# Twenty-four attention steps, and the projections computed between them: single products or heads and rests

## The chip, the cores and the metric

The kernel runs on one core of one Trainium2 chip. The metric is the device time of one execution, in microseconds (us). The engines are named as the profile names them: PE is the matrix engine (TensorE), DVE the vector engine (VectorE), ACT the scalar engine (ScalarE), POOL is GpSimd, and SP (SyncE) issues most transfers. Each takes its own instructions in order, and they wait for each other through semaphores.

## What is computed

A decoder trunk of two layers over 512 rows of 1024 numbers. Only the first part of a layer, the mixer, is touched by the change. Cut to that:

```python
h = rms_norm(x, norm_mix[l])
z = h @ w_in[l]
(g_q, g_k, g_v, g_lr, g_r, d_q, d_k, d_v, i_q, i_k, i_w, c_u) = jnp.split(z, split_at, axis=-1)
o_gla  = rms_norm(gla_chunked(g_q, g_k, g_v, log_a), gla_onorm[l]) * jax.nn.silu(g_r)
o_dsa  = dsa_attention(rms_norm(d_q), rms_norm(d_k), d_v, i_q, i_k, i_w, rel_bias, topk)
o_conv = conformer_conv(c_u, ...)         # a * sigmoid(g), 31 taps over time, layer norm, silu
x = x + concatenate([o_gla, o_dsa, o_conv]) @ w_out[l]
```

After it come a cross-attention and a mixture of experts. `h @ w_in` is in float32. A product with float32 operands can be made directly, or from three products in the format fp32r. For that each operand is written as a head (its value copied to fp32r, by ACT) and a rest (value minus head, a subtraction); head times head, head times rest and rest times head are summed.

## The kernel before, in words

**The projections.** `w_in` is loaded in nine chunks (`CHUNKS`), three at a time in slots of `arena` (`chunk_at(n)` is slot n mod 3). A chunk is computed in jobs (`JOBS`), each with eight parts (c = 0 to 7, blocks of 128 of the 1024 inputs). Chunks 0 and 1 (the index keys and queries) are single float32 products with `hT`, the turned and normalised rows. Chunks 2 to 5 (`SPLIT`: dq, dk, dv, and g for gq and gk) are made from heads and rests: ACT writes the head of the rows `hT_head` and of each chunk `w_head` (`rows_head`, `chunk_head`), POOL subtracts (`rows_rest`, `chunk_rest`; the rest of a chunk takes the place of the chunk itself in its slot), and `split_project` gives PE three products a part. Chunks 6, 7 and 8 (ca and cg for the convolution and its gate; gv; gr, the gate of the linear attention) are single float32 products. `hT_head` lies where `x` was, so `x` is loaded again once chunk 5 is done (SP, L585).

**The steps.** The jobs of chunks 6 to 8 and the small jobs kt, upd and o of the linear attention aren't computed in one piece. They are spread, part by part, over the 24 steps of the sparse attention (4 tiles of rows by 6 heads). In step n PE turns the weights (`turn(n)`, L767), gives two parts, the products of a level of the linear attention (`level_product`, L692 and L707), in even steps the logits of steps n+2 and n+3 (`logits`, L758), the step's other parts, and `values(n-1)` (L776). DVE in its step n masks the logits of n+1 (`masked`, L1078), normalises n (`normalise`, L1088), merges a level, prepares the next (`differences` or `level_queries`), and does taps of the convolution (`conv_tap`, L1097 to L1100). `decay_to_end` (L1136) stands in step FACTORED and `factors` in the next. ACT does the exponentials and takes the jobs out of PSUM (`evacuate`). POOL adds bias and mask (`bm`, L1233 and L1234), up to two steps ahead, and multiplies the levels' keys (`level_keys`, L1223).

**What sets the order.** `LENGTH` holds an estimate for a part of each kind. The first four steps get 6.5 us of it each (`EARLY_US`), and the rest is spread evenly up to step 22. Which step a job ends in follows from this, and so do FACTORED and FIRST_TAP (the step after cg has ended); the taps are spread evenly from FIRST_TAP to step 21.

## Time and profile before

| | us |
|---|---|
| median of 3 runs | 1613.76 |
| lowest, highest | 1610.63, 1616.23 |
| profiled execution, device time | 1611.07 |
| its span in the profile | 1609.2 |
| PE, DVE, ACT, POOL busy | 1518.3, 1172.2, 848.5, 505.1 |
| mean granted clock of PE | 0.966 of full speed |

A busy time says how long an engine had something under way and not whether it bounds the kernel. A float32 product stands in the records as two matmuls. Brackets behind a row of the timeline give the idle time before it and who ended it. Layer 0 has its mixer from about 20 to 333 us, its steps from 150 to 310; layer 1 has the same steps from about 945 to 1107 us. Between the two lie the cross-attention and the experts.

### The profile page before, as it was taken

The page shows a single profiled execution, that of the slowest core. Times are in us where ns is not written, and L with a number is a line of the kernel's source. Part 1 is how long each engine was busy: PE and PEld are TensorE (multiplying, and loading weights), DVE is VectorE, ACT ScalarE, POOL GpSimd, SP SyncE. Part 2 cuts the span into 40 slices and gives each one's busy share as a digit, 9 for nine tenths or more (in the row PEclk, how much of TensorE's full clock was granted, in tenths as well). Part 3 has the DMA queues.
Part 4 walks back from the last instruction along what each step waited for, and adds up shares of the span by engine and source line. Part 5 has one row for each costly group of instructions (what it writes and reads, how often), then busy time and mean ns, then how long its engine had stood idle before and what let it go on. Part 6 is the DMA issues. An engine that isn't in the chain of part 4 may idle for free. (4 is left out here: it accounts for less than half of the span.)

```text
span 1609.2 us, 19743 instructions
## 1 busy us (share of the span) xinstructions
PE 1518.3 (94%) x6478; PEld 1044.6 (65%) x6478; DVE 1172.2 (73%) x1730; ACT 848.5 (53%) x1234; POOL 505.1 (31%) x224
## 2 busy tenths in 40 slices
PE   7999999999898999999899999999998899999996
PEld 3587565545566888877546865655455578877774
DVE  2697499541458999999837965985315599999997
ACT  4642323531537878788464513236125377788881
POOL 3043123100003666553532421321000036555444
PEclk9999989999979999999899999999998899999998
DMA  6243301314017999999641430103140289999994
GB/s 223 79 105 131 117 1 53 131 55 157 1 53 266 392 398 398 399 398 399 234 164 40 113 135 1 53 1 131 55 157 1 69 315 395 398 399 399 399 399 187
DMA packets 151769, 313.74 MB, mean 195 GB/s; under 512 B 33190, under 2 KB 46412, under 8 KB 151516
## 3 DMA queue, kind: packets, MB, share of 16 engines
q1 hardware_dynamic: 140300, 271.39, 46.5%
q0 software_dynamic: 6912, 25.17, 4.1%
q10 hardware_dynamic: 4496, 16.40, 2.5%
q8 instruction: 34, 0.56, 0.1%
q14 instruction: 27, 0.22, 0.0%
HBM read 288.81 MB, written 29.50 MB: 198 GB/s over the span
## 5 line engine op out<-in xcount | busy, mean ns | idle before, releaser
L1806 POOL TENSOR_TENSOR rest_w_down<-arena,head_w_down 128x2048 fp32r<-128x2048 f32 x30 | 189.1, 6304 | 193.8 <-ACT head_w_down L1955 193.8
L645 PE MATMUL ps<-hT,arena 128*128 128x512 f32 x352 | 162.8, 603 | 0.0
L2049 DVE TENSOR_TENSOR rest_w_down<-arena,head_w_down 128x2048 fp32r<-128x2048 f32 x30 | 150.5, 5018 | 14.8 <-ACT head_w_down L1955 14.7
L2049 DVE TENSOR_TENSOR rest_w_gate<-arena,head_w_gate 128x2048 fp32r<-128x2048 f32 x62 | 141.3, 2279 | 11.7 <-remote 11.7
L2049 DVE TENSOR_TENSOR rest_w_up<-arena,head_w_up 128x2048 fp32r<-128x2048 f32 x64 | 143.5, 2282 | 0.4 <-ACT head_w_up L1955 0.4
L1955 ACT ACTIVATE head_w_gate<-arena 128x2048 fp32r<-128x2048 f32 x60 | 114.8, 1918 | 41.4 <-DMA arena<-in_w_gate 40.6
L1955 ACT ACTIVATE head_w_down<-arena 128x2048 fp32r<-128x2048 f32 x60 | 115.0, 1925 | 39.5 <-DMA arena<-in_w_down 38.8
L1955 ACT ACTIVATE head_w_up<-arena 128x2048 fp32r<-128x2048 f32 x64 | 122.3, 1944 | 9.3 <-DMA arena<-in_w_up 9.2
L1740 POOL DMA_INDIRECT xg<-hrows,slot_tok x2 | 4.2, 2121 | 366.5 <-DVE slot_tok L1726 366.5
L1850 PE MATMUL ps<-head_w_gate,xg_head 128*128 128x512 f32 x256 | 105.6, 412 | 9.7 <-DVE xg_rest L2055 9.1
L645 PEld LDWEIGHTS ps<-hT,arena 128*128 128x128 f32 x352 | 63.9, 192 | 69.0 <-issue 68.1
L1850 PE MATMUL ps<-head_w_down,he_head 128*128 128x512 f32 x240 | 99.1, 413 | 5.4 <-DVE rest_w_down L2049 3.2
L1851 PE MATMUL ps<-rest_w_gate,xg_head 128*128 128x512 f32 x256 | 102.1, 399 | 0.0
L1852 PE MATMUL ps<-head_w_gate,xg_rest 128*128 128x512 f32 x256 | 101.8, 398 | 0.0
L1100 DVE SCALAR_TENSOR_TENSOR mixr<-arena,cf,mixr 128x512 f32<-128x512 f32 x120 | 98.4, 820 | 4.3
L1852 PE MATMUL ps<-head_w_up,xg_rest 128*128 128x512 f32 x256 | 99.7, 389 | 0.0
L1850 PE MATMUL ps<-head_w_up,xg_head 128*128 128x512 f32 x256 | 99.6, 389 | 0.0
L1851 PE MATMUL ps<-rest_w_up,xg_head 128*128 128x512 f32 x256 | 99.6, 389 | 0.0
L1852 PE MATMUL ps<-head_w_down,he_rest 128*128 128x512 f32 x240 | 94.1, 392 | 0.0
L1851 PE MATMUL ps<-rest_w_down,he_head 128*128 128x512 f32 x240 | 93.8, 391 | 0.0
L1963 ACT ACTIVATE xg_head<-ps,cf 128x128 fp32r<-128x128 f32 x256 | 69.2, 381 | 39.0 <-PE ps L1841 39.0
L1799 POOL DMA_INDIRECT xg<-hrows,idx x30 | 78.4, 2613 | 22.6 <-POOL idx L1812 22.6
(335 smaller groups left out, 3382.2 us busy)
## 6 DMA issues: line engine op xcount, KB each, us to landing
arena<-in_w_gate SPq DMA_DIRECT2D x64, 1024.0 KB, 10.3
arena<-in_w_up SPq DMA_DIRECT2D x64, 1024.0 KB, 11.0
arena<-in_w_down SPq DMA_DIRECT2D x64, 1024.0 KB, 10.4
arena<-in_w_in SPq DMA_DIRECT2D x10, 1536.0 KB, 6.7
yrows<-yb ACTq DMA_DIRECT2D x30, 512.0 KB, 6.3
arena<-in_w_in SPq DMA_DIRECT2D x4, 2048.0 KB, 7.8
x<-in_x SPq DMA_DIRECT2D x8, 512.0 KB, 13.9
arena<-in_w_in SPq DMA_DIRECT2D x16, 256.0 KB, 4.6
```

The lines of the kernel that those rows point to most:

```text
L645: last = nc.tensor.matmul(ps[n % 2][0:width, :], w[:, c, col:col + width], hT[:, c, :], start=(c == 0), stop=(c == KD - 1))
L1100: do(nc.vector.scalar_tensor_tensor(o, cin[:, i, j:j + S], convw[:, i, j:j + 1], o, ALU.mult, ALU.add))
L1740: gp.indirect_dma_start(out=xg[:, :], out_offset=None, in_=hrows, in_offset=bass.IndirectOffsetOnAxis(ap=slot_tok[:, 0:1], axis=0)).then_i ...
L1799: gp.indirect_dma_start(out=xg[:, :], out_offset=None, in_=hrows, in_offset=bass.IndirectOffsetOnAxis(ap=idx[:, :], axis=0)).then_inc(s_ga ...
L1806: nc.gpsimd.tensor_tensor(wl[2][:, c, :], raw[2][:, c, :], wh[2][:, c, :].bitcast(F32), ALU.subtract)\
L1850: nc.tensor.matmul(out, ah, bh, start=(c == 0), stop=False)
L1851: nc.tensor.matmul(out, ah, bl, start=False, stop=False)
L1852: last = nc.tensor.matmul(out, al, bh, start=False, stop=(c == n - 1))
L1955: nc.scalar.activation(wh[q][:, part(q, j), :], raw[q][:, part(q, j), :], ACT.Copy)\
L1963: last = nc.scalar.activation(xh[:, c, :], ps[4 + half][:, P * (c % 4):P * (c % 4) + P], ACT.Copy, scale=pc("gffn", c))
L2049: nc.vector.tensor_tensor(wl[q][:, c, :], raw[q][:, c, :], wh[q][:, c, :].bitcast(F32), ALU.subtract)\
```

## The change

Chunks 6, 7 and 8 are made from heads and rests too. For want of one large buffer their heads are made in seven pieces: ca, cg, gv_b (parts 5 to 7 of gv), gv_a (parts 0 to 4), gr0, gr1, gr2. Nothing is left in single float32 but chunks 0 and 1.

The rest of the rows is made twice: once as before (`hT_rest1`, for chunks 2 to 4), and once in two halves in the place of `hT` itself, for chunk 5 and later, since the first place is needed for heads. The heads of ca, cg and gv_b are made before the steps, gv_a's in step 1, gr0's in step 4, gr1's in step 10, gr2's in step 11; POOL makes the rests of the first three behind `bm` of step 1, and the others at its steps 5, 7, 13 and 15. `x` is loaded again only after the last part of gr, behind half of `w_out` instead of ahead of it. The lengths of parts become shorter, which moves jobs ahead: cg ends in step 3 (step 4 before), gv in step 9 (11 before), FACTORED and FIRST_TAP are 4 (5 before). Two idle products of PE ahead of layer 1 are gone.

```diff
-        SPLIT = [2, 3, 4, 5]
+        w_head = dict(dq=..., dk=..., dv=..., g=...,
+                      ca=heads_at("ca_head", place_of_sq, KD, CC), cg=heads_at("cg_head", soon, KD, CC),
+                      gv_a=heads_at("gv_head_a", place_of_sq, 5, GH * GV), gv_b=heads_at("gv_head_b", soon + 4 * KD * CC, 3, GH * GV),
+                      gr0=w_rest[8 % NSLOT][:, :, 384:512], gr1=heads_at("gr1_head", place_of_rs, KD, P),
+                      gr2=heads_at("gr2_head", place_of_sq, KD, P))
+        HEADS = ["rows", "dq", "dk", "dv", "g", "ca", "cg", "gv_b", "gv_a", "gr0", "gr1", "gr2"]
+        RESTS = ["rows1", "dq", "dk", "rows_a", "dv", "rows", "g", "ca", "cg", "gv_b", "gv_a", "gr0", "gr1", "gr2"]
...
-            LENGTH = dict(ca=0.87, cg=0.87, gr=0.87, gv=0.65, kt=0.6, upd=0.7, o=1.5)
+            LENGTH = dict(ca=0.69, cg=0.69, gr=0.69, gv=0.52, kt=0.6, upd=0.7, o=1.5)
+            VALUED, GATES = step_of(done("gv") - 1), step_of(done("gv") - 1) - 3
...
-                    sp.wait_ge(sN["proj_done"], BEFORE_STEPS)
+                    sp.wait_ge(sN["proj_done"], done("gr"))
                     for t in range(NT):
...
+                    def split_part(n, c):
...
+                        if c == 0:
+                            pe.wait_ge(sN["heads_in"], HEADS.index(of) + 1)
+                            pe.wait_ge(sN["rests_in"], RESTS.index(of) + 1)
...
+                        for a, (lhs, rhs) in enumerate(pairs):
+                            last = nc.tensor.matmul(o, lhs, rhs, start=(c == 0 and a == 0), stop=(c == KD - 1 and a == 2))
...
+                    def head(of, chunk, c=slice(0, KD), at=None):
...
+                        nc.scalar.activation(dst, chunk_at(chunk)[:, c, at], ACT.Copy).then_inc(sN["heads_in"], 1)
...
+                    rest("dk", 3)
+                    gp.wait_ge(sN["proj_done"], AFTER_IDX)
+                    rows_rest(hT_rest, slice(0, KD // 2))
+                    rest("dv", 4)
+                    rows_rest(hT_rest, slice(KD // 2, KD))
+                    rest("g", 5)
...
                         if n == 1:
+                            rest("ca", 6, at=slice(0, CC))
+                            rest("cg", 6, at=slice(CC, 2 * CC))
+                            rest("gv_b", 7, c=slice(5, KD))
...
+                        if n == 5:
+                            rest("gv_a", 7, c=slice(0, 5))
+                        if n == GATES + 1:
+                            rest("gr0", 8, at=slice(0, P))
+                        if n == VALUED + 4:
+                            rest("gr1", 8, at=slice(P, 2 * P))
+                        if n == VALUED + 6:
+                            rest("gr2", 8, at=slice(2 * P, 3 * P))
...
                         row_turned(pe, 3)
-                        idle_products(2)
```

DVE from the end of its step 4 into its step 5, which begins with the masking of step 6's logits. The line numbers of the changed kernel are higher: L1136 is L1177 there, L1097, L1098 and L1100 are L1138, L1139 and L1141, and the masking L1078 is L1119. Before:

```order
L1107 TENSOR_TENSOR mixg<-arena 128x1024
L1078 ISA scratch,small<-ps,scratch 128x256
L1078 ISA small 128x1
L1080 TENSOR_SCALAR small<-small 128x1
L1087 RECIPROCAL small<-small 128x1
L1088 TENSOR_SCALAR scratch<-scratch,small 128x128
L1131 COPY_PREDICATED arena<-cmask,ps 128x8x32x2
L1115 TENSOR_TENSOR mixg<-arena,mixg 128x128x4
L1136 TENSOR_TENSOR arena<-arena 128x1024
L1097 TENSOR_TENSOR arena<-arena 128x512
L1098 TENSOR_SCALAR mixr<-arena,cf 128x512
L1100 SCALAR_TENSOR_TENSOR mixr<-arena,cf,mixr 128x512 x2
```

The same place of the changed kernel:

```order
L1148 TENSOR_TENSOR mixg<-arena 128x1024
L1177 TENSOR_TENSOR arena<-arena 128x1024
L1138 TENSOR_TENSOR arena<-arena 128x512
L1139 TENSOR_SCALAR mixr<-arena,cf 128x512
L1141 SCALAR_TENSOR_TENSOR mixr<-arena,cf,mixr 128x512 x2
L1119 ISA scratch,small<-ps,scratch 128x256
L1119 ISA small 128x1
L1121 TENSOR_SCALAR small<-small 128x1
L1128 RECIPROCAL small<-small 128x1
L1129 TENSOR_SCALAR scratch<-scratch,small 128x128
L1172 COPY_PREDICATED arena<-cmask,ps 128x8x32x2
L1156 TENSOR_TENSOR mixg<-arena,mixg 128x128x4
```

Five instructions (the decays, the gate of the convolution and its first three taps) have moved from behind the masking of step 6 to ahead of it.

POOL in its steps 13 to 15, before (`arena` 128x1152 is the clearing of the states, L1233 and L1234 are `bm`, L1223 the levels' keys):

```order
L1233 TENSOR_SCALAR scratch<-sel,bfar 128x128
L1234 TENSOR_TENSOR scratch<-sel,toep 128x256
L1233 TENSOR_SCALAR scratch<-sel,bfar 128x128
L1234 TENSOR_TENSOR scratch<-sel,toep 128x256
L1223 TENSOR_TENSOR mixg<-arena,mixg 128x16x32
L1244 MEMSET arena 128x1152
L1233 TENSOR_SCALAR scratch<-sel,bfar 128x128
L1234 TENSOR_TENSOR scratch<-sel,toep 128x256
```

and in the changed kernel (L1277, L1278, L1267 and L1300 there; L1238 is a rest):

```order
L1277 TENSOR_SCALAR scratch<-sel,bfar 128x128
L1278 TENSOR_TENSOR scratch<-sel,toep 128x256
L1238 TENSOR_TENSOR w_rest_77<-arena,gr_head 128x8x128
L1300 MEMSET arena 128x1152
L1277 TENSOR_SCALAR scratch<-sel,bfar 128x128
L1278 TENSOR_TENSOR scratch<-sel,toep 128x256
L1267 TENSOR_TENSOR mixg<-arena,mixg 128x16x32
L1277 TENSOR_SCALAR scratch<-sel,bfar 128x128
L1278 TENSOR_TENSOR scratch<-sel,toep 128x256
L1238 TENSOR_TENSOR w_rest_77<-arena,gr_head 128x8x128
```

The rests of gr1 and gr2 have come behind the `bm` of steps 13 and 15.

## Rows read from the trace of the kernel before

**Rows 1.** The page, section 1: busy time, share, instructions of each engine.

```profile
PE 1518.3 (94%) x6478; PEld 1044.6 (65%) x6478; DVE 1172.2 (73%) x1730; ACT 848.5 (53%) x1234; POOL 505.1 (31%) x224
```

**Rows 2.** Busy us by windows: PE, PEld, DVE, ACT, POOL, PEclk, DMA, GB/s.

```profile
180.00:190.00 10.00, 10.00 (x38) 5.06 (x37) 3.40 (x4) 2.44 (x7) 0.72 (x1) 1.00 0.00 1
...
230.00:240.00 10.00, 9.99 (x52) 6.02 (x50) 9.33 (x19) 3.72 (x9) 4.36 (x5) 1.00 0.00 2
```

**Rows 3.** The same view, one narrow window after TensorE's pause at 200 us.

```profile
204.00:206.00 2.00, 2.00 (x10) 1.95 (x10) 1.90 (x4) 1.53 (x3) 0.00 (x0) 0.50 0.00 0
```

**Rows 4.** Groups by shape, 0 to 420 us: heads on ACT, rests on POOL.

```profile
L1202 POOL TENSOR_TENSOR w_rest<-arena,w_head 128x3072 fp32r<-128x3072 f32 x3 | 20.3, 6770 | 10.0 <-ACT w_head L891 9.9
...
L891 ACT ACTIVATE w_head<-arena 128x3072 fp32r<-128x3072 f32 x3 | 8.3, 2758 | 0.0
```

**Rows 5.** Timeline of PE: start, us, instruction; products of either kind in the projections.

```profile
37.30 20.87 PE L645 MATMUL ps<-hT,arena 128*128 128x512 f32 x48
...
74.02 0.40 PE L628 MATMUL ps<-hT_head,w_rest 128*128 128x512 f32 x1
...
74.25 0.39 PE L628 MATMUL ps<-hT_rest,w_head 128*128 128x512 f32 x1
...
111.12 0.33 PE L628 MATMUL ps<-w_rest,hT_head 128*128 128x384 f32 x1
...
111.29 0.33 PE L628 MATMUL ps<-w_head,hT_rest 128*128 128x384 f32 x1
...
197.48 2.20 PE L648 MATMUL ps<-arena,hT 128*128 128x384 f32 x6
```

**Rows 6.** Timeline of PE: the transposes of steps 4 and 6.

```profile
187.76 0.33 PE L767 MATMUL ps<-cf,scratch 128*128 128x128 f32 x1
...
201.88 0.44 PE L767 MATMUL ps<-cf,scratch 128*128 128x128 f32 x2 [1.83 <-DVE scratch L1088]
```

**Rows 7.** Timeline of DVE: steps 5 and 6, and where step 7 begins.

```profile
192.36 0.42 DVE L1078 CUSTOM_DVE_ANT_0 scratch<-ps,scratch 128x256 f32<-128x256 f32 x1 [6.72 <-PE ps L758]
...
196.04 1.23 DVE L1136 TENSOR_TENSOR arena<-arena 128x1024 f32<-128x1024 f32 x1
...
198.61 1.54 DVE L1100 SCALAR_TENSOR_TENSOR mixr<-arena,cf,mixr 128x512 f32<-128x512 f32 x2
...
210.32 0.42 DVE L1078 CUSTOM_DVE_ANT_0 scratch<-ps,scratch 128x256 f32<-128x256 f32 x1
```

**Rows 8.** Timeline of DVE: its pauses behind step 6, layer 0, last one layer 1.

```profile
263.59 0.56 DVE L1078 CUSTOM_DVE_ANT_0 scratch<-ps,scratch 128x384 f32<-128x384 f32 x1 [0.97 <-PE ps L758]
...
276.14 0.69 DVE L1078 CUSTOM_DVE_ANT_0 scratch<-ps,scratch 128x512 f32<-128x512 f32 x1 [0.33 <-PE ps L758]
...
288.17 0.69 DVE L1078 CUSTOM_DVE_ANT_0 scratch<-ps,scratch 128x512 f32<-128x512 f32 x1 [1.46 <-PE ps L758]
...
307.39 0.17 DVE L1087 RECIPROCAL small<-small 128x1 f32<-128x1 f32 x1 [2.34 <-ACT scratch L944]
...
1085.74 0.69 DVE L1078 CUSTOM_DVE_ANT_0 scratch<-ps,scratch 128x512 f32<-128x512 f32 x1 [3.13 <-PE ps L758]
```

**Rows 9.** Timeline of POOL, one multiplication of the levels' keys.

```profile
225.53 1.60 POOL L1223 TENSOR_TENSOR mixg<-arena,mixg 128x512 f32<-128x512 f32 x1
```

**Rows 10.** Timeline of DVE, four taps of the convolution beside it.

```profile
226.04 4.01 DVE L1100 SCALAR_TENSOR_TENSOR mixr<-arena,cf,mixr 128x512 f32<-128x512 f32 x4
```

**Rows 11.** The page, section 5: rests on POOL and DVE in the experts.

```profile
L1806 POOL TENSOR_TENSOR rest_w_down<-arena,head_w_down 128x2048 fp32r<-128x2048 f32 x30 | 189.1, 6304 | 193.8 <-ACT head_w_down L1955 193.8
...
L2049 DVE TENSOR_TENSOR rest_w_down<-arena,head_w_down 128x2048 fp32r<-128x2048 f32 x30 | 150.5, 5018 | 14.8 <-ACT head_w_down L1955 14.7
...
L2049 DVE TENSOR_TENSOR rest_w_gate<-arena,head_w_gate 128x2048 fp32r<-128x2048 f32 x62 | 141.3, 2279 | 11.7 <-remote 11.7
```

**Rows 12.** Timeline of PE: last idle products before layer 1, and its first projection.

```profile
813.22 1.89 PE L388 MATMUL ps<-ones 128*128 128x512 f32 x4
...
815.57 7.07 PE L645 MATMUL ps<-hT,w_first 128*88 128x512 f32 x16 [0.46 <-PEq L1757]
```

More of the change, by code:

```diff
@@ L479, in program, with weights_of, rest_of @@
             NJ = len(JOBS)
+            def weights_of(name, i):
+                return {"gq": "g", "gk": "g", "gv": "gv_a", "gr": f"gr{i}"}.get(name, name)
+            def rest_of(chunk):
+                return hT_rest1 if chunk < 5 else hT_rest
             def k_of(chunk):
@@ L581, in _ @@
                     sp.dma_start(one_head, A["heads"].rearrange("p (n c) -> p n c", c=P)).then_inc(sN["wor_in"], 16)
-                    sp.wait_ge(sN["proj_done"], BEFORE_STEPS)
+                    w = A["w_out"][bass.ds(l, 1)].rearrange("o (c p) n -> p (o c) n", p=P)
+                    sp.wait_ge(sN["proj_done"], done("gv"))
+                    sp.dma_start(view(arena, SLOT, 4, D), w[:, GC:GC + 4, :]).then_inc(sN["wor_in"], 16)
+                    sp.wait_ge(sN["proj_done"], done("gr"))
                     for t in range(NT):
@@ L585, in _ @@
                         sp.dma_start(x[:, t, :], rows).then_inc(s_xt[t], 16)
-                    w = A["w_out"][bass.ds(l, 1)].rearrange("o (c p) n -> p (o c) n", p=P)
-                    sp.wait_ge(sN["proj_done"], done("gv"))
-                    sp.dma_start(view(arena, SLOT, 4, D), w[:, GC:GC + 4, :]).then_inc(sN["wor_in"], 16)
                     sp.wait_ge(sN["proj_done"], done("o"))
@@ new lines, in split_part @@
+                        of, at = weights_of(name, i), slice(col, col + width)
+                        if c == 0:
+                            pe.wait_ge(sN["heads_in"], HEADS.index(of) + 1)
+                            pe.wait_ge(sN["rests_in"], RESTS.index(of) + 1)
+                        wl = w_rest[k_of(chunk)][:, c, at]
+                        if name == "gv":
+                            wh = w_head["gv_a"][:, c, :] if c < 5 else w_head["gv_b"][:, c - 5, :]
+                        elif name == "gr":
+                            wh = w_head[of][:, c, :]
+                        else:
+                            first = CC if name == "cg" else 0
+                            wh = w_head[of][:, c, col - first:col - first + width]
@@ L631, in project @@
+                        return last
                     def project(n, chunks=range(KD)):
@@ L916, in _ @@
                                              scale=ID ** -0.5).then_inc(sN["relu_done"], 1)
-                    chunk_head(1)
+                    act.wait_ge(sN["dots_done"], len(DOTS))
+                    head("dk", 3)
                     for n in range(6):
@@ L924, in _ @@
                         if n == 2:
-                            chunk_head(2)
-                    chunk_head(3)
+                            act.wait_ge(sN["proj_done"], done("dq"))
+                            head("dv", 4)
+                    act.wait_ge(sN["proj_done"], done("dk"))
+                    head("g", 5)
                     evacuate(AFTER_IDX + 6)
@@ L936, in _ @@
                         do(nc.scalar.activation(ps[QK_SUMS[n]], ps[QK_SUMS[n]], ACT.Exp, scale=-0.5), "sums_root", wait=False)
+                    head("ca", 6, at=slice(0, CC))
                     for n in range(AFTER_IDX + 8, BEFORE_STEPS):
                         evacuate(n)
+                        if n == AFTER_IDX + 9:
+                            act.wait_ge(sN["proj_done"], done("dv"))
+                            head("cg", 6, at=slice(CC, 2 * CC))
+                        if n == AFTER_IDX + 10:
+                            head("gv_b", 7, c=slice(5, KD))
                     def exps(n):
@@ L980, in _ @@
                             evacuate(job)
+                            if job == done("ca") - 1:
+                                head("gv_a", 7, c=slice(0, 5))
+                        if n == GATES - 2:
+                            head("gr0", 8, at=slice(0, P))
+                        if n == VALUED + 1:
+                            act.wait_ge(sN["proj_done"], done("gv"))
+                            head("gr1", 8, at=slice(P, 2 * P))
+                        if n == VALUED + 2:
+                            head("gr2", 8, at=slice(2 * P, 3 * P))
                         if n and n % AH == 0:
@@ L1213, in _ @@
                                                    channel_multiplier=1), "causal_done")
-                    for m in range(1, len(SPLIT)):
-                        chunk_rest(m)
+                    rest("dk", 3)
[4 more added lines that the diff above has]
+                    rest("g", 5)
                     def level_keys(v):
```

79 lines of the change are left out of this document (34 added, 45 removed).

## The prediction

> **What bounds the kernel now.** The page comes first: PE is busy for 94% of the span [rows 1]. That invites the sum "less work on PE, so much less time", and the stages have to be looked at before it is believed. The change touches the steps of the mixer alone, 160 of some 800 us in each layer. There the busy times by windows tell two stages apart. From step 0 to the end of step 5 (153 to 196 us of layer 0) PE has no pause and DVE waits: at 180 to 190 us PE is busy for 10.00 us and DVE for 3.40 [rows 2]. Behind that DVE is full too: 9.33 of 10 us at 230 to 240 [rows 2], what is missing being the gaps of some 0.03 us between instructions. The timeline of DVE gives the proof. Before the masking of step 6's logits, at 192.36, it waited for 6.72 us [rows 7]; from there to its last tap at 303 us I find only five pauses for PE's logits: 0.97, 0.33 and 1.46 us [rows 8] and two smaller. So PE sets the time of steps 0 to 5, and DVE that of steps 6 to 21, with PE close behind it. At 201.88 it is PE that waits 1.83 us for DVE [rows 6]. The reader should see in the rows of DVE whether a bracket stands behind the masking: none means that a quicker PE wins nothing there.
>
> **What the change takes from PE.** A float32 product of 512 columns costs 20.87 us / 24 = 0.87 us, the row's 48 records being 24 products; three fp32r products start 0.23 us apart, 0.69 in all [rows 5]. So 0.18 us a part, for the 7 jobs of ca, cg and gr with 8 parts each: 10.1 us. At 384 columns it is 2.20 / 3 = 0.73 against 3 x 0.17 = 0.51 us [rows 5], 0.22 for each of 32 parts: 7.0 us. That makes 17 us a layer and 34 over both, all of it on PE. How much of it reaches the end is the question.
>
> **Heads and rests ahead of the steps.** ACT's head of 128x3072 takes 2.76 us, POOL's rest 6.77, so 0.9 and 2.2 ns an element [rows 4]. The second rest of the rows (two halves of 2048, 4.5 us each), those of ca and cg (2048, 4.5 each) and of gv_b (1152, 2.5) are 20.5 us of POOL. They fall between its existing rests and the steps, where it stands idle until gk is out, and PE asks for none before the steps. ACT's three heads (4.7 us) stand between takings-out that PE is a job away from needing. Nothing, as long as that cover holds. If POOL were late with ca, PE would wait in step 0 and each us would count.
>
> **The first stretch, steps 0 to 4.** PE is given 6.5 us of parts in each of the first four steps by both kernels. Before these were 30 parts (of ca and cg) of 0.87, 26.1 us; now they are 40, all 32 of ca and cg and 8 of gv: 32 x 0.69 + 8 x 0.51 = 26.2 us. So step 4 starts where it did, at 187.76 [rows 6]. But by then cg is done. Ahead of the logits of step 6 stand two parts of gv (1.0 us) instead of two of cg (1.7): the masking of step 6 starts 0.7 us earlier. And the five instructions that moved ahead of it, from 196.04 to 198.61 + 1.54 = 200.15, are 4.1 us [rows 7] that now lie in DVE's old wait of 6.72. **These 4.8 us a layer are the main gain**, since DVE is without pause behind them.
>
> **The pauses behind.** PE has about 0.8 us less to do in each later step, so the pauses of 0.97 and 0.33 should close: 1.3 us. That of 1.46 comes from two jobs o ahead of the logits [rows 8], which stay. At the end DVE waits 2.34 us for ACT [rows 8], which takes out o of head 3; PE reaches that job earlier, with gr2's eight parts 0.18 us shorter each: I take 1.2 of 1.4. Together 2.5 us a layer.
>
> **What POOL costs DVE.** The rests of gr0, gr1 and gr2 (1024 elements, 2.2 us each) now run beside DVE's full stretch. Four taps beside the multiplication of the keys took 4.01 us [rows 10], where two alone took 1.54 [rows 7]: 0.93 us more, for the 1.1 us that POOL's instruction (225.53 to 227.13) [rows 9] still had to go. The experts show it too: a rest of 2048 on DVE takes 5.02 us while POOL makes one (itself 6.30), and 2.28 otherwise [rows 11]. Bounds for a rest of 2.2 us are 1.0 (its end beside instructions that don't mind) and 2.2; I take 1.0 for gr0, part of which meets DVE's early reads of PSUM, and 1.7 for each of the others, 4.4 us a layer. The rest of gv_a (1920, 4.2 us) should run where DVE waits for PE: 0.3, up to 2 if it comes late.
>
> The Trainium skill, "SBUF — State Buffer", says on contention that VectorE and GpSimd take a shared pair of ports as an exclusive lock for a whole instruction, and the other blocks fully. The taps agree (0.93 of 1.1 us lost); by that rule alone the three rests would cost 6.6 us instead of 4.4, and the forecast would be 4.4 us later.
>
> **What the clock costs.** After the pause at 200 us the granted clock is 0.50 at 204 to 206 us [rows 3], 1.2 GHz, and PE is back at full only some 10 us later. DVE hardly notices today. With the change PE waits longer there (its step 5 is 1.1 us shorter, DVE's a little longer) and the logits of step 8, in a step at half speed, are due some 2.5 us sooner. I take 1.0 us a layer; none and 3 are the bounds, 3 being what one more such stretch would cost later, half of a step of 5.5 us of PE's work at least.
>
> **Small terms.** The heads of gv_a and gr in the steps are 1.7 + 3 x 0.9 us on ACT, half idle there: nothing. `x`'s load (2 MB) now waits for gr, ahead of `w_out`'s second part, due some 25 us later: nothing. The two idle products end at 813.22 + 1.89, the projection starts at 815.57 [rows 12]; 0.5 us may go.
>
> **The sum.** A layer: 4.8 + 2.5 - 4.4 - 0.3 - 1.0 = 1.6 us; I add 0.7 for layer 1, where one pause is 3.13 us instead of 1.46 [rows 8]. 2 x 1.6 + 0.7 + 0.5 = 4.4 us. From the profiled execution's 1611.07 that gives 1606.7; it lies 2.7 us below the median of the three runs, and I put the forecast at **1606.5 us**. A measurement of this kernel tells 0.3% (4.8 us) from no change, so the forecast stands just on the edge.
>
> **Rivals.** (1) *PE is the bound after all*, the pauses of DVE being absent because the two are coupled through two steps of logits: then most of the 34 us shows, less 2 x 4.4 for the rests: about 1586. For it speaks rows 1, against it the brackets missing in DVE's timeline. (2) *The moved work pays in full, the rests do little*, since POOL's rests find DVE in instructions that don't mind: 2 x (4.8 + 2.5 - 1.5) + 1, about 1598. (3) *It is eaten*: rests by their whole 2.2 us (2 x 2.2 more), nothing gained at the tails (2 x 1.2): 1611 to 1613. (4) *Slower: the clock.* With PE's work a step down by 0.8 us it waits for DVE in most steps, by 1 to 2 us. If a pause of that size lets the clock fall as the one of 1.83 us did, PE is half as fast for 10 us, in which it has 5.5 us of work for each 6.5 us step: 11. Its slack to DVE's next need of logits is about 1 us, so each fall costs some 3 us. It decides from two falls a layer beyond the one of today: 2 x (2 x 3) on top of the forecast, 1618.
>
> The Trainium skill, "TensorE: Matmul & The Clock Gate", has a section on oscillation by short pauses between groups of matmuls. It bears on (4), and pauses of 0.5 to 1 us in the trace, where the clock stayed at 1.00, speak against it so far.
>
> (5) *The change doesn't do what it says*: a head or rest late in the steps holds PE, and with it ACT and POOL behind their waits. POOL reaches each of its rests two steps or more ahead of PE's use. Small, and within (3) or (4).
>
> **How the numbers follow.** The forecast with its surroundings (1602 to 1610) 40%; (1) 7%; (2) and what lies between, 1594 to 1602, 20%; (3) 19%; (4) with (5) 14%. Leaving out (1) and half of (4), the range is 1595 to 1616, 2.7 us of which are the spread of the runs. Faster by over 0.3%: (1), (2) and half of the forecast, 0.47. Within: the other half and most of (3), 0.37. Slower: 0.16.
>
> **What would show it.** In the profile after, the products of gr, ca and cg start 0.23 us apart. In DVE's timeline its wait ahead of step 6's masking is 2 to 3 us instead of 6.72, with the decays ahead of it, and step 7 begins near 208 instead of 210.32. Taps beside POOL's rests take over 4 us for four. PE's waits for DVE grow to 1 us and more in most steps. The steps end 1 to 3 us earlier. Wrong would be: a PE that still has no pause from 210 to 240 us with DVE waiting behind it (then rival 1 or 4), stretches of half clock after 215 us, or a PE that waits for POOL at the first part of a job.

## The result: slower by 0.5%

Eight executions of the changed kernel have a median of 1626.06 us (1622.68 to 1630.48), those of the kernel before beside them 1616.14 us (1610.63 to 1622.61). The ratio is 1.0053, with a 95% interval of 1.0032 to 1.0074. The forecast was a gain of 4.4 us; by the ratio the kernel lost 8.6 us (9.9 by the two medians), and the time lies above the range. The profiled execution of after is its fastest, 1622.68 us with a span of 1620.8.

The first section of the page of after, to be held against [rows 1]:

```profile
PE 1501.7 (93%) x6650; PEld 1087.3 (67%) x6650; DVE 1193.4 (74%) x1730; ACT 865.3 (53%) x1248; POOL 586.9 (36%) x242
```

PE lost 17 us of busy time (though more of its work now runs at half clock), POOL gained 82, and DVE, with the same 1730 instructions, gained 21. The last number is the one to stop at: the same instructions take longer.

The steps of layer 0, from the first transposition of step 0 to the last of step 23, take 163.9 us where they took 155.7; in layer 1 164.9 against 159.0. In the windows view (columns as in [rows 2], the clock third from the end) the stretches behind step 6 read, first in the kernel before:

```profile
200.00:220.00 20.00, 18.17 (x70) 11.58 (x70) 18.99 (x33) 5.33 (x15) 3.44 (x4) 0.74 0.00 0
220.00:250.00 30.00, 28.87 (x158) 18.84 (x158) 28.16 (x47) 9.21 (x22) 9.74 (x11) 1.00 0.20 71
250.00:300.00 50.00, 46.09 (x231) 27.35 (x230) 44.36 (x85) 17.71 (x40) 15.93 (x17) 1.00 0.00 1
```

and then in the changed kernel:

```profile
200.00:220.00 20.00, 14.00 (x60) 11.90 (x60) 17.47 (x31) 3.38 (x9) 3.49 (x5) 0.57 0.01 1
220.00:250.00 30.00, 26.26 (x149) 21.15 (x148) 27.73 (x44) 10.46 (x24) 12.87 (x13) 0.86 0.19 71
250.00:300.00 50.00, 42.78 (x239) 32.10 (x238) 42.23 (x74) 15.88 (x37) 16.42 (x17) 0.88 0.00 1
```

DVE, which should have been full here, is less busy than before, and the clock fell in all three stretches. PE's timeline in the changed kernel gives the pauses in front of the falls. These are transpositions (the line was L767 before) that wait for DVE's normalisation, of steps 6, 11 and 18:

```profile
206.00 0.69 PE L794 MATMUL ps<-cf,scratch 128*128 128x128 f32 x2 [7.00 <-DVE scratch L1129]
...
242.56 0.69 PE L794 MATMUL ps<-cf,scratch 128*128 128x128 f32 x2 [2.97 <-DVE scratch L1129]
...
289.09 1.11 PE L794 MATMUL ps<-cf,scratch 128*128 128x128 f32 x4 [3.99 <-DVE scratch L1129]
```

The first answers to the 1.83 us of [rows 6]. DVE's timeline shows what held DVE in step 5, and how it waits for PE's logits in return:

```profile
186.07 1.22 DVE L1177 TENSOR_TENSOR arena<-arena 128x1024 f32<-128x1024 f32 x1
...
192.64 0.42 DVE L1119 CUSTOM_DVE_ANT_0 scratch<-ps,scratch 128x256 f32<-128x256 f32 x1 [2.41 <-PE ps L785]
...
195.18 2.63 DVE L1156 TENSOR_TENSOR mixg<-arena,mixg 128x512 f32<-128x512 f32 x1
197.85 1.65 DVE L1181 TENSOR_TENSOR arena<-arena 128x1024 f32<-128x1024 f32 x1
199.53 1.12 DVE L1183 COPY ebl<-arena 128x8 f32<-128x8 f32 x1
...
213.30 0.42 DVE L1119 CUSTOM_DVE_ANT_0 scratch<-ps,scratch 128x256 f32<-128x256 f32 x1 [1.62 <-PE ps L785]
...
295.88 0.69 DVE L1119 CUSTOM_DVE_ANT_0 scratch<-ps,scratch 128x512 f32<-128x512 f32 x1 [4.15 <-PE ps L785]
...
307.17 0.69 DVE L1119 CUSTOM_DVE_ANT_0 scratch<-ps,scratch 128x512 f32<-128x512 f32 x1 [1.41 <-PE ps L785]
```

The decays' difference (L1177) stands at 186.07 now, in DVE's old wait, and step 6's masking (192.64) waits 2.41 us in place of 6.72: the part of the forecast called its main gain is there. Behind it the queries' product (L1156) takes 2.63 us, where 0.69 is its shortest in this trace, and the copy of eight columns (L1183) 1.12, where it takes 0.17 in e2, e3 and e10. POOL's timeline has the other side:

```profile
194.92 2.35 POOL L1238 TENSOR_TENSOR w_rest<-arena,w_rest 128x1024 fp32r<-128x1024 f32 x1 [13.36 <-ACT w_rest L914]
...
198.49 2.13 POOL L1267 TENSOR_TENSOR mixg<-arena,mixg 128x512 f32<-128x512 f32 x1
...
238.66 2.70 POOL L1238 TENSOR_TENSOR w_rest<-arena,gr_head 128x1024 fp32r<-128x1024 f32 x1 [3.73 <-ACT gr_head L914]
...
250.25 2.35 POOL L1238 TENSOR_TENSOR w_rest<-arena,gr_head 128x1024 fp32r<-128x1024 f32 x1
```

POOL stood for 13.36 us at gate 0's rest, because ACT makes that head behind the exponentials of step 4's factors; the level's keys stood behind it. Then rest, `bm` and keys ran in one go through DVE's step 5.

**Three theories** come out of this. *Lock*: a rest on POOL holds DVE's instructions for its whole length. *Order*: with the shorter lengths the planner gives steps 16, 17 and 18 of the steps 1, 0 and 6 parts (4, 1 and 4 before), because the output products may not start ahead of step 18; PE pauses in step 17, and the pile in 18 makes the logits of step 20 late. *Clock*: PE's pauses let the clock fall, and PE at half speed is late with logits.

### The profile page after: what moved, and what is told of

The parts are those of the page before. It is cut to its first block and busy times, and to the rows that moved or that the text cites. A ratio compares the mean times of both kernels' runs of the same rounds, so it can differ in the third digit from the quotient of the medians.

```text
span 1620.8 us, 20149 instructions
## 1 busy us (share of the span) xinstructions
PE 1501.7 (93%) x6650; PEld 1087.3 (67%) x6650; DVE 1193.4 (74%) x1730; ACT 865.3 (53%) x1248; POOL 586.9 (36%) x242
## 5 line engine op out<-in xcount | busy, mean ns | idle before, releaser
L1862 POOL TENSOR_TENSOR rest_w_down<-arena,head_w_down 128x2048 fp32r<-128x2048 f32 x30 | 202.2, 6740 | 179.6 <-ACT head_w_down L2010 179.6
L2104 DVE TENSOR_TENSOR rest_w_down<-arena,head_w_down 128x2048 fp32r<-128x2048 f32 x30 | 155.9, 5197 | 9.8 <-ACT head_w_down L2010 9.6
L659 PE MATMUL ps<-hT_head,w_rest 128*128 128x512 f32 x288 | 116.2, 414 | 0.0
L1141 DVE SCALAR_TENSOR_TENSOR mixr<-arena,cf,mixr 128x512 f32<-128x512 f32 x120 | 96.8, 807 | 4.3
L2110 DVE SCALAR_TENSOR_TENSOR xg_rest<-ps,cf,xg_head 128x128 fp32r<-128x128 f32 x256 | 68.8, 337 | 2.3 <-ACT xg_head L2018 2.3
```

The lines of the kernel that those rows point to most:

```text
L659: last = nc.tensor.matmul(o, lhs, rhs, start=(c == 0 and a == 0), stop=(c == KD - 1 and a == 2))
L1141: do(nc.vector.scalar_tensor_tensor(o, cin[:, i, j:j + S], convw[:, i, j:j + 1], o, ALU.mult, ALU.add))
L1862: nc.gpsimd.tensor_tensor(wl[2][:, c, :], raw[2][:, c, :], wh[2][:, c, :].bitcast(F32), ALU.subtract)\
L2104: nc.vector.tensor_tensor(wl[q][:, c, :], raw[q][:, c, :], wh[q][:, c, :].bitcast(F32), ALU.subtract)\
L2110: last = nc.vector.scalar_tensor_tensor(xl[:, c, :], ps[4 + half][:, P * (c % 4):P * (c % 4) + P], pc("gffn", c), xh[:, c, :].bitcast(F32) ...
```

## The experiments

Each kernel is the changed one but for the edit shown, unless its text says otherwise. All ratios are to the kernel before, run beside it. The medians of the kernel before were 1615.75, 1617.64, 1617.87 and 1618.10 us in the four sets (e1 to e4, e5 to e8, e9 to e12, e13 and e14).

### e1: the pauses filled

```diff
                         if n >= 1:
                             values(n - 1)
+                        for _ in range({5: 22, 10: 9, 17: 13}.get(n, 0)):
+                            nc.tensor.matmul(ps[3][:, 3 * P:4 * P], ones[:, :], ones[:, :], start=True, stop=True)
```

> The changed kernel with 44 idle 128x128 products a layer on TensorE, in its three longest pauses of the steps: 22 ahead of the transposition of step 6 (pause 7.00 us), 9 ahead of step 11's (2.97 us), 13 ahead of step 18's (3.99 us). Theory 'clock': the pauses let the granted clock fall (0.50 from 202 to 218 us, 242 to 254 and 286 to 292), the products at half clock make the logits late, and VectorE waits 9.55 us for them behind step 6 where it waited 3.46 before. Then here the clock stays above 0.9 from 202 to 300 us, the waits for the logits fall to about 3.5 us, and the kernel is 10 to 12 us faster than the changed one: 1614 to 1616 us, ratio 0.999 to 1.000 to the kernel before. Theory 'lock' (GpSimd's rests hold VectorE up, the clock only follows): the clock stays up too, but VectorE is paced by its own slower instructions, and the time moves by 0 to 4 us: ratio 1.003 to 1.005. If the order of the work alone makes the logits late: the waits stay at 9 us and the ratio at 1.005 or above.

1.0025 (1.0001 to 1.0049). The clock of the three stretches above:

```profile
200.00:220.00 20.00, 18.09 (x97) 15.72 (x96) 18.02 (x31) 3.51 (x10) 3.43 (x4) 0.74 0.00 1
220.00:250.00 30.00, 27.83 (x173) 21.82 (x171) 28.18 (x45) 11.97 (x27) 15.44 (x13) 0.95 0.20 71
250.00:300.00 50.00, 44.96 (x288) 34.88 (x290) 44.62 (x81) 18.04 (x41) 16.70 (x18) 1.00 0.02 4
```

It stayed up behind 220, and between 200 and 220 it is at the 0.74 of the kernel before. In the profiled execution the steps are 5.4 and 3.8 us shorter than in the changed kernel; by the ratios 4.5 us of all are won, with intervals that overlap. Both lie below the 10 to 12 us of the clock's theory, the second just above the 0 to 4 of the lock's. The profile gives the clock a share; by the ratios about half of the loss stays, but its size is not shown.

### e2: gate 0's head two steps earlier

```diff
-                        if n == GATES - 2:
+                        if n == GATES - 4:
                             head("gr0", 8, at=slice(0, P))
```

> ScalarE makes the head of gate 0 two steps earlier (behind step 2 in place of step 4), so that GpSimd finds it ready and doesn't stand 13.36 us at its rest with bm and the level's keys queued behind it. Theory 'pile-up': rest, bm and keys then run apart from VectorE's queries of the level (2.63 us beside them, 0.69 alone), step 5 on VectorE falls from 11.66 to 9.5 to 10 us, TensorE's pause ahead of step 6's transposition from 7.0 to about 5 us, and the steps end 2 us a layer sooner: 3 to 6 us of all, ratio 1.002 to 1.0035. Rival: the rest only meets other instructions of VectorE, and the ratio stays at 1.005.

1.0021 (1.0002 to 1.0040). POOL makes that rest at 180.66 without a wait, the queries' product finds it gone, and DVE's step 5 takes 8.7 us (191.65 to 200.38) in place of 11.7; the pause of 7.00 us becomes 3.87. DVE's busy time from the masking of step 6 to that of step 22 falls by 3.1 us in each layer. As expected: by the ratios the late instruction on ACT cost some 5 us, with intervals that overlap.

### e3: no gate rests

```diff
                         elif name == "gr":
-                            wh = w_head[of][:, c, :]
+                            wh = wl = w_head[of][:, c, :]
...
-                        if n == GATES + 1:
-                            rest("gr0", 8, at=slice(0, P))
-                        if n == VALUED + 4:
-                            rest("gr1", 8, at=slice(P, 2 * P))
-                        if n == VALUED + 6:
-                            rest("gr2", 8, at=slice(2 * P, 3 * P))
```

> The rests of the three gate blocks are not made, and TensorE multiplies by the heads once more in their place: as many products, no rest on GpSimd beside the steps behind gv's (this leaves out that part of the gates' accuracy). What is taken away is the three rests of about 2.4 us a layer. Theory 'lock' (VectorE's two-input instructions stand for the whole of a rest, the Trainium skill's SBUF page says so of its port): 6.6 us a layer go, 13 us of all, and with the shorter pauses perhaps 4 more: 1609 to 1613 us, ratio 0.995 to 0.998. My prediction's price of 4.4 us a layer: 9 us, ratio 0.9995. Theory 'clock' alone: the pauses of 7.0, 2.97 and 3.99 us stay and so do the falls of the clock; VectorE waits for TensorE in place of GpSimd, and the kernel gains 0 to 4 us, ratio 1.003 to 1.005.

0.9969 (0.9948 to 0.9991). PE multiplies by the heads once more in their place, so this kernel leaves out a part of the gates' accuracy. Against the changed kernel that is 0.84%, 13.6 us or 6.8 a layer for three rests, with an interval from about 4.4 to 9.2. It speaks for the price by the lock; my 4.4 lies at its edge. The profile agrees with the larger price: DVE's busy time in the same stretch falls by 7.7 and 7.2 us. The pauses of 2.97 and 7.00 went to 1.10 and 3.88 with them, that of 3.99 stayed: it has another cause.

### e4: the old lengths

```diff
-            LENGTH = dict(ca=0.69, cg=0.69, gr=0.69, gv=0.52, ...
+            LENGTH = dict(ca=0.87, cg=0.87, gr=0.87, gv=0.65, ...
-            VALUED, GATES = step_of(done("gv") - 1), step_of(done("gv") - 1) - 3
+            VALUED, GATES = step_of(done("gv") - 1), 6
```

> The table of lengths back at 0.87 and 0.65, all else as changed (heads and rests where they were in the steps but for gr1 and gr2, which move two steps back with the end of gv's projections). It spreads the parts of the projections as before: 4 and 1 of them in steps 16 and 17, where the changed kernel has 1 and 0, and 8 in the first steps in place of 10. Theory 'clock through the order of work': the pause ahead of step 18's transposition (3.99 us) goes below 1.5, that ahead of step 6's falls from 7.0 to about 5, VectorE's waits for logits from 9.55 to about 5 us, and 3 to 5 us a layer come back: 1616 to 1620 us, ratio 1.000 to 1.0025. Rival 'lock': the same rests run beside VectorE, ratio 1.004 to 1.006.

1.0003 (0.9985 to 1.0021), better than the changed kernel by 8 us. The mechanism expected was hardly there: ahead of step 18's transposition PE still waits 2.98 us, and DVE 5.06, 2.83 and 3.02 us for logits. So this run says only that the table matters; it mixes too many moves (gate 0's head comes ahead of the exponentials here as well) to say why.

### e5: output products from step 17

```diff
-            EARLY, EARLY_US, LAST_FILLED, FIRST_O = 4, 6.5, 22, 18
+            EARLY, EARLY_US, LAST_FILLED, FIRST_O = 4, 6.5, 22, 17
```

> The changed kernel with the heads' output products allowed from step 17 in place of 18, so that steps 16 to 18 hold 1, 2 and 4 parts where the changed kernel has 1, 0 and 6. Theory 'hole in the order': the pause of 3.99 us ahead of step 18's transposition and the 4.15 us that VectorE waits for the logits of step 20, behind the pile of six, go below 1.5 us each, the clock stays at 1.00 from 286 to 296 us (0.66 in the changed kernel), and the steps end 3 to 4 us a layer sooner: ratio 1.001 to 1.003. Rival: VectorE sets the pace there anyway (its rows are back to back between the waits), and the wait only moves to the next logits: ratio 1.0045 to 1.006.

1.0006 (0.9984 to 1.0028). The masking that had waited 4.15 us, in the timeline of DVE:

```profile
292.46 0.69 DVE L1119 CUSTOM_DVE_ANT_0 scratch<-ps,scratch 128x512 f32<-128x512 f32 x1 [0.57 <-PE ps L785]
```

The pause ahead of step 18 is 0.94 us, and the steps are 3.6 and 3.3 us shorter. One digit gives back 0.47%, nearly the whole loss.

### e6: the kernel before with the new lengths

```diff
-            LENGTH = dict(ca=0.87, cg=0.87, gr=0.87, gv=0.65, ...
+            LENGTH = dict(ca=0.69, cg=0.69, gr=0.69, gv=0.52, ...
```

> The kernel before with nothing changed but the table of lengths, 0.69 and 0.52 in place of 0.87 and 0.65: the same order of parts as in the changed kernel, with plain products and no rest on GpSimd in the steps. Theory 'the order costs by itself': the hole in steps 16 and 17 and the pile behind it are here too, VectorE waits for the logits of step 20 by 2 to 4 us, and TensorE, whose parts are 0.23 us longer each, is late in steps 0 to 3: 2 to 4 us a layer slower, ratio 1.002 to 1.005. Rival 'the rests are the whole cost': without them the five instructions of VectorE that the order moves ahead of step 6 are a gain of their own, ratio 0.996 to 0.999.

1.0039 (1.0025 to 1.0054). No head, no rest, and three quarters of the loss: DVE's wait for the logits of step 20 is here too.

```profile
294.61 0.69 DVE L1078 CUSTOM_DVE_ANT_0 scratch<-ps,scratch 128x512 f32<-128x512 f32 x1 [4.18 <-PE ps L758]
```

Step 6's masking starts at 198.76, 6.4 us later than before, since ten and nine parts at the old price stand in the first steps. This is the part that the heads and rests pay for: in the changed kernel it starts at 192.64.

### e7 and e8: mends together

e7 holds the edits of e2 and e5 and puts back the two idle products behind `row_turned(pe, 3)`. e8 has all of it and

```diff
-                        if n == GATES + 1:
+                        if n == GATES - 1:
                             rest("gr0", 8, at=slice(0, P))
...
+                        for _ in range({5: 12, 10: 9}.get(n, 0)):
+                            nc.tensor.matmul(ps[3][:, 3 * P:4 * P], ones[:, :], ones[:, :], start=True, stop=True)
```

> The changed kernel with three things at once: gate 0's head two steps earlier (alone 1.0021 to the kernel before, where the changed kernel has 1.0053), the output products from step 17, and the two idle products behind the last turned row back. If the causes are separate: 1.0021 less 3 to 4 us a layer for the order, that is 0.997 to 0.999 by the sum; if they share one critical stretch, or the last steps are VectorE's: 1.000 to 1.002. The idle products are expected at nothing (within 1 us), since the weights' product behind them waits 1.64 us for its queue in the changed kernel and 0.46 before.

> The same three, and gate 0's rest two steps earlier (GpSimd, step 5 in place of 7, before VectorE sets the pace), and 12 and 9 idle products in TensorE's pauses ahead of the transpositions of steps 6 and 11 (3.87 and 2.98 us with the earlier head). Theory 'clock': the fall between 203 and 218 us is gone or shorter, and 1 to 2 us a layer come on top of the version without: ratio 0.995 to 0.998. Rival: the products that the clock makes late are not waited for there, ratio equal to the version without, within 0.001.

e7: 0.9954 (0.9933 to 0.9974). e8: 0.9960 (0.9941 to 0.9978). The causes add up, and the mended kernel beats the one before. Filling the pauses on top moved nothing in the ratios, which leave room for some 4 us either way: the rival of e8 held. In the profiled executions the clock of 220 to 250 us is 0.79 in e7 and 0.95 in e8, but the filling need not be the cause: e10, which has the steps of e7 without filling, has 0.94 there.

### e9: the mended order without gate rests

The edits of e7 and of e3; the same part of the gates' accuracy is left out.

> The version with three mends (gate 0's head two steps earlier, output products from step 17, two idle products back; 0.9954) with the gates' rests not made, TensorE multiplying by the heads once more in their place (this leaves out that part of the gates' accuracy). It prices the rests where the order no longer has a hole. Theory 'lock', the whole length of a rest: gate 1's and 2's (2.35 and 2.70 us by the trace) lie in VectorE's stretch, 4.6 us a layer less, 9 us of all, ratio 0.988 to 0.991. My prediction's price of 1.7 us a rest: 3.4 us a layer, ratio 0.991 to 0.993. If the waits for logits set the end there: under 4 us of all, ratio 0.993 to 0.995.

0.9889 (0.9862 to 0.9916), 0.65% below e7 and 0.82% below e10: 5 to 7 us a layer, with intervals of some 3 us each way. This is the price of two rests and not of three, since with the early head gate 0's rest ran ahead of the stretch (at 183.50 us in e10). They last 5.05 us in the changed kernel, and e9 lies in the range of the lock. The rows give less: DVE's busy time in the stretch is 3.5 to 4.7 us a layer lower than in e7 and e10. The same stretch of each kernel, from the masking of step 6 to that of step 22, by the windows view; before, changed, e9:

```profile
192.36:298.44 106.08, 99.21 (x482) 61.23 (x482) 97.34 (x170) 36.17 (x82) 31.11 (x34) 0.95 0.06 21
```

```profile
192.64:307.17 114.53, 96.58 (x525) 75.56 (x525) 100.03 (x165) 37.37 (x85) 39.83 (x37) 0.84 0.07 23
```

```profile
194.31:295.56 101.25, 88.29 (x525) 68.44 (x525) 92.38 (x165) 36.77 (x84) 31.33 (x34) 0.95 0.08 26
```

The third busy time is DVE's. Without rests it is 92.38, 5.0 below before: 4.0 of it are the five moved instructions (five records fewer). The changed kernel has 100.03, 7.7 more than e9 with the same instructions, and 14.5 us without work where before had 8.7. The table lists more of the same view.

| kernel | stretch | DVE busy | DVE not busy | clock | ratio |
|---|---|---|---|---|---|
| before | 106.1 | 97.3 | 8.7 | 0.95 | 1 |
| changed | 114.5 | 100.0 | 14.5 | 0.84 | 1.0053 |
| e1 pauses filled | 109.1 | 98.8 | 10.3 | 0.94 | 1.0025 |
| e3 no gate rests | 105.8 | 92.4 | 13.5 | 0.92 | 0.9969 |
| e5 outputs from 17 | 110.9 | 100.1 | 10.8 | 0.86 | 1.0006 |
| e6 before, new lengths | 108.5 | 92.7 | 15.9 | 0.92 | 1.0039 |
| e10 mended | 104.4 | 95.9 | 8.6 | 0.93 | 0.9971 |
| e11 mended, quarters | 103.0 | 94.4 | 8.6 | 0.95 | 0.9920 |
| e12 before, mended order | 104.0 | 92.7 | 11.3 | 0.95 | 0.9993 |
| e13 changed, quarters | 109.7 | 96.9 | 12.8 | 0.89 | 1.0015 |

### e10 to e12: the idle products, shorter rests, and the control

e10 is e7 without the idle products. e11 is e10 with each gate rest in four instructions:

```diff
+                        q = 4 if of in ("gr0", "gr1", "gr2") else 1
+                        m = (c.stop - c.start) // q
+                        for j in range(q):
+                            cj = slice(c.start + m * j, c.start + m * j + m) if q > 1 else c
+                            hj = slice(m * j, m * j + m)
+                            last = nc.gpsimd.tensor_tensor(w_rest[k_of(chunk)][:, cj, at], chunk_at(chunk)[:, cj, at],
+                                                           w_head[of][:, hj, 0:at.stop - at.start].bitcast(F32), ALU.subtract)
+                        last.then_inc(sN["rests_in"], 1)
```

e12 is the kernel before with the edits of e6 and e5.

> The three mends without the two idle products behind the last turned row. Expected: within 0.001 of the version with them (0.9954), so that the order and the head carry all of the gain: 0.9948 to 0.9965. If the idle products are worth something on their own (a product queue that is ready sooner), 0.997 or above.

> As the version without idle products, with each gate rest made by four instructions of a quarter's columns. Theory 'lock by the instruction': VectorE gets in between the quarters, its single stand falls from 2.1 us (its product with the level's queries took 3.39 us beside a rest, 1.23 to 1.26 alone) to some 0.6, but the sum over a rest stays near its length, since it meets several instructions; with GpSimd's start costs the ratio is the same to 0.001 higher. Theory 'only the instruction that is caught pays': less than half of the price remains, 1.2 us a rest or 5 us of all come back, ratio 0.992 to 0.993.

> The kernel before with the new lengths (alone 1.0039) and the output products from step 17: the mended order without any heads and rests of the last chunks. Theory 'the hole was the order's cost': 3 to 4 us a layer come back, ratio 0.998 to 1.000; what the mended changed kernel (0.9954) is below that is then what the heads and rests bring. If the new lengths' cost lies in the first steps (10 and 9 parts of 0.46 us products in steps 0 and 1), 1.002 to 1.004.

e10: 0.9971 (0.9952 to 0.9990). That is 0.17% above e7, with intervals that overlap, so nothing is shown of the idle products either way. But e7 and e10 have the same steps, and their profiled executions differ in the clock, one in each layer. The stretch in layer 0 and in layer 1, of e7 and then of e10:

```profile
192.24:299.33 107.09, 93.98 (x525) 72.77 (x525) 97.11 (x165) 36.43 (x84) 36.23 (x36) 0.89 0.07 25
991.42:1096.98 105.56, 89.93 (x525) 69.92 (x525) 96.92 (x165) 36.88 (x84) 37.08 (x36) 0.94 0.07 25
```

```profile
194.50:298.92 104.42, 89.80 (x525) 69.59 (x525) 95.87 (x165) 36.95 (x84) 37.65 (x36) 0.93 0.07 25
986.01:1093.15 107.14, 93.99 (x525) 72.77 (x525) 97.13 (x165) 36.51 (x84) 36.28 (x36) 0.89 0.07 25
```

In layer 0 e10 has 0.93 for e7's 0.89 and is 2.7 us shorter; in layer 1 e7 has 0.94 for e10's 0.89 and is 1.6 us shorter. DVE is without work for 10.0 us in both stretches at 0.89 and for 8.6 in the others. So a lower clock goes with lost time in the mended order too; the filling of e8 did not bring it back.

e11: 0.9920 (0.9895 to 0.9945), the best of the kernels that make every rest. Gate 2's rest shows how the two engines share. In the changed kernel DVE starts its product 0.04 us behind POOL's rest of 2.35 us (250.25, above), and takes 3.40 us where the shortest of this line take 1.22 to 1.25:

```profile
250.29 3.40 DVE L1148 TENSOR_TENSOR mixg<-arena 128x1024 f32<-128x1024 f32 x1
```

In e10, which e11 has to be held against, the same rest comes a little behind DVE's product. It takes 3.23 us itself, and DVE loses its time in the four taps, which take 3.12 elsewhere. POOL, then DVE:

```profile
247.37 3.23 POOL L1238 TENSOR_TENSOR w_rest<-arena,gr_head 128x1024 fp32r<-128x1024 f32 x1
```

```profile
248.41 5.10 DVE L1141 SCALAR_TENSOR_TENSOR mixr<-arena,cf,mixr 128x512 f32<-128x512 f32 x4
```

With quarters the taps take 4.51 us. POOL, then DVE:

```profile
243.89 5.00 POOL L1243 TENSOR_TENSOR w_rest<-arena,gr_head 128x256 fp32r<-128x256 f32 x4
```

```profile
243.31 1.58 DVE L1148 TENSOR_TENSOR mixg<-arena 128x1024 f32<-128x1024 f32 x1
244.93 4.51 DVE L1141 SCALAR_TENSOR_TENSOR mixr<-arena,cf,mixr 128x512 f32<-128x512 f32 x4
```

DVE's loss at this rest is 0.35 + 1.39 = 1.7 us, in place of 2.2 in the changed kernel and 2.0 in e10, and POOL's four quarters last 5.00 us. By busy time DVE wins 1.4 us over e10 in layer 0 (95.9 to 94.4), most of it in the step of gate 1's rest, and 3.1 in layer 1 (97.1 to 94.0); the ratios say 4 us a layer with an interval of some 2.5 each way. So the direction is shown, and the size only roughly.

e12: 0.9993 (0.9972 to 1.0013). The digit that mended the changed kernel by 0.47% mends this one by 0.46%: the hole belongs to the lengths, not to the rests. It is also the control for the whole idea. In the mended order heads and rests bring 0.9971 / 0.9993, 0.2% (within the intervals; 0.4% by e7), with whole rests, and 0.7% with quarters.

### e13 and e14: quarters alone, and eighths

e13 is the changed kernel with e11's quarters and nothing else. e14 is e10 with

```diff
+                        q = {"gr0": 8, "gr1": 8, "gr2": 8, "gv_a": 5}.get(of, 1)
```

> The changed kernel (1.0053) with nothing but the three gate rests made by four instructions of a quarter's columns each. In the version with the mended order quarters gave 0.992 where whole rests gave 0.9971, 5 us a layer less of it than no rests at all (0.9889) leaves. If that is the same cost here, and separate from the hole in the order: 8 us less, ratio 0.999 to 1.001. If the hole in steps 16 to 18 and the late head of gate 0 (GpSimd's wait of 13.36 us, with its bm and keys behind it) hide it: 1.003 to 1.005, and the waits for logits grow by what VectorE saves.

> The mended order (gate 0's head two steps earlier, output products from step 17) with the gate rests in eight instructions each and the last part of gv's rest in five. If what VectorE loses is the length of one caught instruction of GpSimd at a time, another 0.5 us a rest goes: ratio 0.990 to 0.992. If from quarters on both engines share the access evenly (GpSimd's four quarters took 5.00 us beside VectorE, 3.21 elsewhere), nothing more is won: 0.992 to 0.993, with GpSimd's rests longer.

e13: 1.0015 (0.9997 to 1.0033), 0.38% or 6.1 us better than the changed kernel. DVE's busy time in the stretch falls by 3.1 us in layer 0 and 3.5 in layer 1, which is as much as the ratios give. e14: 0.9947 (0.9925 to 0.9970), no better than quarters. DVE is busy for 93.0 us in the stretch, the least of all with rests, but it waits more (12.8 us without work, one wait of 3.24 for the logits of step 16 among them), and the two rests last 4.76 and 4.79 us. The wait of 3.24 us ends at 267.76. Ahead of it PE paused for 1.91 us at step 14, and its clock fell; from 262 to 270 us PE has no pause and half the clock:

```profile
262.00:270.00 8.00, 8.00 (x29) 5.61 (x28) 4.51 (x10) 0.71 (x2) 1.24 (x2) 0.50 0.00 0
```

So a fall can make logits late in the mended order too. What the longer rests cost beside it is open.

## Why the prediction was wrong

**Right.** Products of the split chunks start 0.23 us apart; the heads and rests ahead of the steps cost at most 0.5 us (step 0 starts at 153.56 instead of 153.10); the decays and first taps moved into DVE's old wait, which is 2.41 us ("2 to 3"). That part of the main gain is there: 4.0 of the 5.0 us that DVE is busy less in e9, against the 4.1 of the forecast. Most of the 0.7 us that step 6 should start earlier is missing: its masking starts 0.28 us later, 0.18 earlier when counted from step 0. DVE's pauses of 0.97 and 0.33 us, for the logits of steps 16 and 18, closed. Rival 1, PE as the bound, is out.

**The term of the rests was too small.** "I take 1.0 for gr0 ... and 1.7 for each of the others, 4.4 us a layer." It measured 6.8 by the ratios (e3), and 7.7 and 7.2 as busy time of DVE in the two layers. e2 divides that. Gate 0's rest, with what stood behind it, cost 3.1 us in place of 1.0. Gates 1 and 2 cost 4.6 and 4.1 together in place of 3.4, and in the mended order 3.5 to 4.7. The bound of 2.2 a rest had been worked out and then left for a guess that DVE would often be in instructions that don't mind. In step 5 the queries, the factors and even the copy of eight columns stood. The Trainium skill, "SBUF — State Buffer", in its section "Who interferes with whom", has the shared ports held for a whole instruction and the other engine blocked. The row at 250.29 agrees: 2.17 of 2.35 us lost. The 6.6 us that the prediction worked out for this rule and set aside are nearer to e3 than its 4.4, but only together with what gate 0's late rest brought.

**Gate 0's rest was placed by the wrong engine.** The prediction looked at when POOL reaches its rests and when PE needs them, not at when ACT makes the head. "POOL reaches each of its rests two steps or more ahead of PE's use" is true, and useless: POOL waited 13.36 us there with `bm` and the keys in its queue, so that three of its instructions met DVE's step 5 at once. Of the 7.7 us 3.1 are this; e2 prices it at 5 us of all.

**The order was not looked at.** "PE has about 0.8 us less to do in each later step" took the parts to be spread evenly. The table's shorter lengths and the fixed first step of the output products leave 1, 0 and 6 parts in steps 16 to 18. Two pauses closed as forecast, and so did most of the tail (its wait for ACT went from 2.34 to 0.52), but the pause that was to stay, 1.46 us for the logits of step 20, became 4.15. Waits of 1.62 us for step 8, 0.68 for step 10, 1.39 for step 14 and 1.41 for step 22 stand where 0.30 (step 10) and 0.40 (step 22) were; e5 takes away that of step 20 (0.57) and leaves these. The counts could have been worked out from the table and the planner's loop without a chip. The hole is worth 0.47% in the changed kernel (e5) and 0.46% in the kernel before with the new table (e6 to e12).

This step and the late head are what turned the forecast over: with both mended and nothing else the ratio is 0.9971 (e10), where the forecast's 4.4 us are 0.9973. That the two agree so closely is in part luck, since the rests cost more than forecast even there.

**The clock's term was low where it mattered.** It was 1.0 us a layer, bounds 0 and 3; e1 says 2.3 by the ratios and up to 4.6 by the profiled steps where the order is broken. Where it is mended e8's ratio shows nothing, and the stretches of e7 and e10 say 1.6 to 2.7 us between 0.89 and 0.93 or 0.94. Rival 4 had the sign, and it asked for two falls a layer beyond the one of today, which is what came. But by e1's ratio its mechanism has about half of the loss, and each fall stands behind a pause with a cause of its own. Nor does the length of one pause tell whether the clock falls. In the kernel before PE waits 2.42 us ahead of step 18, and its clock is 1.00 from 282 to 292 us:

```profile
283.28 0.66 PE L767 MATMUL ps<-cf,scratch 128*128 128x128 f32 x4 [2.42 <-DVE scratch L1088]
```

```profile
282.00:292.00 10.00, 8.72 (x52) 5.98 (x53) 8.09 (x17) 5.60 (x12) 4.08 (x4) 1.00 0.00 0
```

Its 1.83 us ahead of step 6 were followed by 0.50, and the prediction reasoned from these alone. The Trainium skill, "TensorE: Matmul & The Clock Gate", describes such falls, from short pauses between groups of products, in its section "A second HAM failure mode: psum-queue depth-cycling", and the trace has them.

The balance of layer 0 from step 6 to 22: 5.0 gained (4.0 by the moved instructions), 7.7 lost to POOL, 5.8 more without work, 8.5 in all. In the profiled executions the loss at the end of layer 0's steps is 8.7 us and 10.0 at the end of layer 1's; between the layers this execution got back 4.6 us (634.0 for 638.6 from the last step to the first, the other versions mostly 637 to 639), at a clock of 0.94 in place of 0.87 from 400 to 480 us. No run shows that to be the change's merit, and layer 1 adds 5.9 of its own.

## What to carry to other kernels

When work moves to an engine that shares a port with the one that sets the pace, price it near its whole length, with what queues behind it, and look for the step in which the pacing engine waits anyway; if there is none, cut it into a few shorter instructions. Follow a moved instruction's inputs to the engine that makes them, and name what queues behind it while it waits. A table of lengths that drives a planner is part of the change: write out the parts of every step before and after, and look for empty steps.

## What was not expected of the hardware

Four quarters of a rest cost DVE less than the whole, and POOL more: 5.00 us for what takes 2.35 to 3.23 as one instruction beside DVE, and the kernel gains 0.4 to 0.5% by it. A copy of 128x8 elements took 1.12 us beside POOL, 0.17 alone, so a short instruction with one input can stand too. And the same steps ran at different clocks in the two layers of one execution (e7 0.89 and 0.94, e10 0.93 and 0.89), and the stretch at the lower clock is 1.6 to 2.7 us longer than the same layer's in the other kernel.
